# A decoder trunk of two layers: where the value projection's last groups are computed around the RWKV-7 recurrence

## The reference

```python
r = xr @ w_r;  k = xk @ w_k;  v = xv @ w_v          # 256x2048 @ 2048x2048 each
decay = exp(-exp(w_log));  g = sigmoid(xg @ g1) @ g2
def step(state, (r, w, k, v, a, b)):                # 32 heads of 64 channels, 256 tokens
    state = state * w + (state @ a) b^T + v k^T
    return state, state @ r
y = group_norm(scan(step)) + bonus(r, k, v)
out = (y * g) @ w_o
```

## Time and profile before

| | us |
|---|---|
| median of 3 runs | 2485.27 |
| lowest and highest | 2484.48 and 2485.36 |
| span of the profiled execution, first to last instruction | 2481.7 |
| TensorE busy in it | 2444.9 |

### The profile page before, as it was taken

How to read it: one execution, slowest core, us unless ns; L and a number is a source line. 1 busy time by engine, 2 the same in 40 slices (tenths; PEclk the granted TensorE clock), 3 DMA queues, 4 the chain that set the end, 5 groups by cost and what they waited for, 6 DMA issues and landing times.

```text
span 2481.7 us, 39434 instructions
## 1 busy us (share of the span) xinstructions
PE 2444.9 (99%) x15550; PEld 2003.2 (81%) x15550; DVE 1410.0 (57%) x1743; ACT 1074.4 (43%) x1347; POOL 126.0 (5%) x166
## 2 busy tenths in 40 slices
PE   8999999999999999999999999999999999999997
PEld 5888788877888888888887788888788888888886
DVE  6688566676744454454446544666745445454445
ACT  4454355444444444443334344453544444443332
POOL 1000235420000000000000000000000000000000
PEclk9999999999999999999999999999999999999999
DMA  7556411255666666665665565445566666666564
GB/s 233 179 195 205 136 42 38 66 208 188 196 192 188 186 193 186 188 188 193 193 195 198 195 193 188 143 167 190 170 187 192 188 186 193 186 194 221 189 194 143
DMA packets 225435, 440.87 MB, mean 178 GB/s; under 512 B 13472, under 2 KB 23744, under 8 KB 224224
## 3 DMA queue, kind: packets, MB, share of 16 engines
q1 hardware_dynamic: 221760, 417.38, 54.1%
q0 software_dynamic: 3552, 21.73, 2.6%
HBM read 436.96 MB, written 2.10 MB: 177 GB/s over the span
## 4 chain that ended last, share of the span: by engine, by line
PE 94%; DVE 3%; ACT 1%; issue 1%; DMA 1%; POOL 0%; DVEq 0%; ACTq 0%; SPq 0%; POOLq 0%
PE ps L595 25%; PE ps L597 25%; PE ps L596 25%; PE ps L892 3%; PE ps L1075 1%; PE ps L775 1%; PE ps L785 1%; PE ps L1103 1%; PE ps L622 1%; PE ps L624 1%; PE ps L623 1%; PE ps L882 1%; PE ps L836 1%; DVE wlo L1684 1%; PE ps L740 1%
## 5 line engine op out<-in xcount | busy, mean ns | idle before, releaser
L1246 ACT CAST whi<-raw 128x1024 fp32r<-128x1024 f32 x735 | 772.5, 1052 | 1145.9 <-PE ps L597 1080.1
L1684 DVE TENSOR_TENSOR wlo<-raw,whi 128x1024 fp32r<-128x1024 f32 x549 | 670.1, 1225 | 622.2 <-ACT whi L1246 620.3
L595 PE MATMUL ps<-whi,ahi 128*128 128x512 f32 x2172 | 851.5, 392 | 2.8 <-DVE wlo L1684 2.8
L597 PE MATMUL ps<-whi,alo 128*128 128x512 f32 x2172 | 845.6, 389 | 0.0
L596 PE MATMUL ps<-wlo,ahi 128*128 128x512 f32 x2172 | 845.1, 389 | 0.0
L595 PEld LDWEIGHTS ps<-whi,ahi 128*128 128x128 f32 x2172 | 407.8, 188 | 87.6 <-DVE wlo L1684 3.6
L597 PEld LDWEIGHTS ps<-whi,alo 128*128 128x128 f32 x2172 | 407.7, 188 | 85.5
L596 PEld LDWEIGHTS ps<-wlo,ahi 128*128 128x128 f32 x2172 | 407.9, 188 | 84.4 <-issue 1.0
L2015 DVE TENSOR_TENSOR wlo<-raw,whi 128x1024 fp32r<-128x1024 f32 x193 | 236.2, 1225 | 249.4 <-ACT whi L1246 247.4
L595 PE MATMUL ps<-whi,hThi 128*128 128x512 f32 x656 | 255.4, 389 | 0.0
L597 PE MATMUL ps<-whi,hTlo 128*128 128x512 f32 x656 | 255.2, 389 | 0.0
(11 more groups left out here) (317 smaller groups left out, 1933.8 us busy)
## 6 DMA issues: line engine op xcount, KB each, us to landing
raw<-w_up SPq DMA_DIRECT2D x176, 512.0 KB, 3.6
raw<-w_down SPq DMA_DIRECT2D x176, 512.0 KB, 4.0
raw<-w_gate SPq DMA_DIRECT2D x170, 512.0 KB, 3.6
raw<-w_k SPq DMA_DIRECT2D x32, 512.0 KB, 3.8
raw<-w_r SPq DMA_DIRECT2D x32, 512.0 KB, 4.4
raw<-w_v SPq DMA_DIRECT2D x32, 512.0 KB, 3.7
raw<-w_o SPq DMA_DIRECT2D x32, 512.0 KB, 4.8
raw<-kv_v SPq DMA_DIRECT2D x32, 512.0 KB, 3.7
```

The source lines that it names most:

```text
L595: mm(o, hi[:, k, tok], whi[:, s, k2, :], start=(k == 0), stop=False)
L597: last = mm(o, lo[:, k, tok], whi[:, s, k2, :], start=False, stop=(k == kt - 1))
L1246: nc.scalar.copy(whi[:, s], src).then_inc(hi_done, 1)
L1684: V.tensor_tensor(wlo[:, s], src, whi[:, s].bitcast(F32), ALU.subtract).then_inc(split_done, 1)
```

## The change

SOLID becomes 3: a third job in the split form makes value groups 4 and 5 ahead of the recurrence. It takes job number 10 of a phase that is planned with 12 jobs but only 11 jobs' chunks. The counts on the two pairs of banks are evened out by a signal from ScalarE's first Exp of the decays. EARLY becomes 6, so 2 value groups and 8 gate groups remain in plain units: 96 in place of 160. The 20 units ahead of slot 0 stay; the 76 in the slots are dealt out anew, where 140 were. Slot 7 keeps its row. The copies out of bank 3 move to the places that fit the new order.

```diff
--- before.py
+++ after.py
@@ -40,7 +40,7 @@
 KC = 2
 RING = 4
 PLAIN = 3
-SOLID = 2
+SOLID = 3
 FK = 4
 FU = FK * 2
 CJ = KT // KC
@@ -51,19 +51,19 @@
 CHUNK = 64
 PAIRS = D // P
 GROUPS = PAIRS // 2
-EARLY = GROUPS // 2
+EARLY = 2 * SOLID
 LATE = GROUPS - EARLY
-TURNS = [("value", 4), ("value", 5), ("gate", 0), ("gate", 1), ("value", 6), ("value", 7)] + [("gate", g) for g in range(2, GROUPS)]
+TURNS = [("value", 6), ("gate", 0), ("gate", 1), ("value", 7)] + [("gate", g) for g in range(2, GROUPS)]
 UNITS = {"value": KT * TT, "gate": 2 * TT}
-SOME = {"state1": 2, "inner3": 1, "outer3": 2, "outer4": 2, "inner5": 3, "outer5": 4}
+SOME = {"state1": 1, "inner3": 1, "outer3": 1, "outer4": 1, "inner5": 1, "outer5": 2}
 FILL = (
-    {"inner1": 3, "outer1": 2, "inner2": 2, "state1": 3, "inner3": 2, "outer3": 3, "outer4": 2, "inner5": 3, "outer5": 4},
-    SOME,
-    {"state1": 1, "inner3": 1, "outer3": 2, "outer4": 2, "inner5": 4, "outer5": 4},
+    {"outer1": 1, "inner2": 1, "state1": 2, "inner3": 2, "outer3": 3, "outer4": 3},
+    {"outer3": 2, "inner5": 2},
+    {"state1": 1, "outer3": 1, "outer4": 2, "inner5": 2, "outer5": 2},
     SOME,
     SOME,
-    {"state1": 2, "inner3": 2, "outer3": 3, "outer4": 2, "inner5": 3, "outer5": 4},
-    {"inner1": 2, "outer1": 2, "inner2": 2, "state1": 4, "inner3": 2, "outer3": 4, "outer4": 4, "outer5": 4},
+    SOME,
+    {"state1": 2, "inner3": 1, "outer3": 2, "outer4": 2, "outer5": 4},
     {"inner1": 4, "outer1": 2, "inner2": 2, "state1": 2, "inner3": 2, "outer3": 2, "inner4": 2, "outer4": 2, "inner5": 2},
 )
 WHOLE = 4
@@ -118,11 +118,11 @@
 
 PH = {}
 _c = _j = 0
-for _name, _jobs, _per in (("proj", 10, CJ), ("wo", NJ, CJ), ("up0", 2 * FB, CJ), ("down0", NJ, CF), ("kvq", 12, CJ),
+for _name, _jobs, _per in (("proj", 12, CJ), ("wo", NJ, CJ), ("up0", 2 * FB, CJ), ("down0", NJ, CF), ("kvq", 12, CJ),
                            ("ao", NJ, CJ), ("up1", 2 * FB, CJ), ("down1", NJ, CF)):
     assert _c % RING == 0 and _j % 2 == 0
     PH[_name] = (_c, _j)
-    _c += _jobs * _per - (WHOLE if _name == "wo" else 0)
+    _c += _jobs * _per - {"proj": CJ, "wo": WHOLE}.get(_name, 0)
     _j += _jobs
 CHUNKS = _c
 LANDED = {PH[n][0] + RING + e: e for n in ("up0", "kvq", "up1") for e in range(PLAIN)}
@@ -992,8 +992,10 @@
                 job(c + CJ, j // 2, 1, KT, ahi, alo)
                 if n < 2:
                     jobs(c + 2 * CJ, j + 2, NJ - 2, KT, ahi, alo)
+                else:
+                    job(c + 2 * CJ, j // 2 + 1, 0, KT, ahi, alo)
             for b in range(2):
-                pe.wait_ge(bank_free[b], 6)
+                pe.wait_ge(bank_free[b], 7)
             transposes_of(0)
             fill(6)
             for a in range(2):
@@ -1291,7 +1293,9 @@
                 if g:
                     act.wait_ge(nat_done, g)
                 ci = ps[:, 4].rearrange("p (t c) -> p t c", t=TT)
-                A(PC[:, g % 3].rearrange("p l c -> p (l c)"), ps[:, 6, 0:8], ACT.Exp)
+                first = A(PC[:, g % 3].rearrange("p l c -> p (l c)"), ps[:, 6, 0:8], ACT.Exp)
+                if g == 0:
+                    first.then_inc(bank_free[1], 1)
                 A(E[:, 0], ci, ACT.Exp)
                 A(E[:, 1], ci, ACT.Exp, scale=-1.0).then_inc(cum_read, 1)
 
@@ -1335,8 +1339,8 @@
             project_first(0, K_, {1: 0, 2: 1})
             project_first(1, R_, {0: 2, 1: 3})
             project_first(2, V_, {})
-            act.wait_ge(bank_free[0], 6)
-            act.wait_ge(bank_free[1], 6)
+            act.wait_ge(bank_free[0], 7)
+            act.wait_ge(bank_free[1], 7)
 
             def turned(g, a):
 
@@ -1436,8 +1440,6 @@
                 outer(s, 2)
                 if s == 7:
                     keep_gate(5)
-                if s in (0, 5):
-                    keep({0: 4, 5: 6}[s])
                 outer(s, 3)
                 if s:
                     outputs(s - 1)
@@ -1449,17 +1451,17 @@
                 if s == 7:
                     for g, bank in ((0, 4), (1, 6), (2, 5)):
                         keep_zt(g, bank)
-                if s in (2, 6):
-                    keep({2: 5, 6: 7}[s])
+                if s in (0, 6):
+                    keep({0: 6, 6: 7}[s])
                 if more:
                     turned(s + 1, 1)
                 if s == 2:
-                    keep_gate(0)
+                    keep_gate(1)
                 outer(s, 5)
                 if more:
                     first(s + 1)
-                if s in (2, 6):
-                    keep_gate({2: 1, 6: 2}[s])
+                if s in (1, 6):
+                    keep_gate({1: 0, 6: 2}[s])
                 if more:
                     for a in (1, 0):
                         value_part(s + 1, a)
@@ -1804,7 +1806,7 @@
             for b, asides in enumerate((parts_of(2), parts_of(3), [lambda: bonus(0), lambda: None, lambda: bonus(1)])):
                 splits(NJ * CJ, b, asides)
             splits_and_mix(2, 3)
-            for b, asides in enumerate(([lambda: None, lambda: None, lambda: bonus(2)], [lambda: bonus(3)])):
+            for b, asides in enumerate(([lambda: None, lambda: None, lambda: bonus(2)], [lambda: bonus(3)], [])):
                 splits(2 * NJ * CJ, b, asides, 4 if b < SOLID - 1 else 2)
 
             def blank(g):
```

## The result

The change makes the kernel slightly slower: 2492.76 us (median of 10 runs, 2490.17 to 2494.40) against 2487.03 us (median of 10), a ratio of 1.0025 with a 95% interval of 1.0017 to 1.0033, that is +4 to +8 us. I had forecast +1.2 us (2486.5) and "same"; the sign of the difference was right, its size was not, and it is clear of no change. The 2486.5 stood on the median of three runs of the kernel before, 2485.27; on the 2487.03 of ten, my +1.2 us would be 2488.2, and the miss is 4.5 us.

What follows compares the result with a forecast made beforehand. TensorE, busy 99% of the span, was taken as the bound. Job +21.8 us less 20.6 given back (of 29.7 removed) made +1.2 us on 2485.27, so 2486.5 us, range 2481 to 2493, "same" at 0.75.

Steps and rivals of the forecast that it cites:

- Added job, 21.8 us: Ahead of the recurrence: third split job, 96 matmuls at 227 ns from start to start, its splits and loads hidden, adds 21.8 us.
- all behind it moves as a block: At the border behind the last half job and after the recurrence: everything shifts together, cost 0, bound 0 to 1.3 us.
- Removed work, 29.7 us: In the recurrence: 64 plain units at 0.43 us plus 11 vanished groups at 0.2 us, 29.7 us of TensorE's time.
- 0.2 us for each of 11 groups: In the recurrence: each group of plain units that vanishes whole saves TensorE 0.2 us beside its units.
- New waits with a releaser, 9.1 us: In the recurrence: of 29.7 us removed, 20.6 is given back and the other 9.1 become short waits of TensorE.
- What I took back for GpSimd: Slots 4 and 5: GpSimd's products for the next group's transposes come late, 0.1 and 0.3 us taken off the gain.
- Two pauses ... taken as unchanged: In runs of small matmuls in the recurrence: TensorE pauses of 1.35 and 0.76 us without releaser stay, bound 2.1 us either way.
- TensorE-bound everywhere: Rival, recurrence: removed work is given back in full, 2477.4 us, or 2482 half way; chance 0.15.
- Clock: Rival: more waits drop TensorE from 2.4 to 1.2 GHz; one slot at the lower level gives 2508 us; chance 0.03.
- The turns: Rival, slot ends (inner5 and outer5): ScalarE and VectorE queues bind, 6.8 us booked there is lost, 2493.3 us; chance 0.15.
- my own signs: Recurrence forecast at 201.8 us; under 197 would mean steps paid for in full, over 206 would mean the turns.
- The 3.6 us between span and time: Whole kernel before: three-run median 2485.27 exceeds the profile's span 2481.7 by 3.6 us, taken as present in every run.

## Why the prediction was wrong

- **Added job, 21.8 us:** 21.2 in the change, 21.4 alone. Right. That all behind it moves as a block: right, 0 at the border and 1979.9 us behind the last outer step in both.
- **Removed work, 29.7 us:** 27.05. The 0.43 us a unit was right (27.5 for 64); the 0.2 us for each of 11 groups was mis-sized. I took the drawn distance between a run of units and its neighbours for a cost, and the work that fell leaves nothing for it. This is 2.65 of the missing 5.9 us.
- **New waits with a releaser, 9.1 us:** 8.2 (1.25 to 9.4). Right in sum, and at the places named: masks at inner 5 and value products behind the copies. The mask wait after inner 5 is 0.29 us in slots 3 to 5; slots 1, 4 and 5 gave, without pauses, 3.0, 2.5 and 3.1 of 2.7, 2.4 and 3.0, slot 3 only 1.9 of 2.5. Not foreseen: the outputs' copy in front of the transposes (0.36 to 0.39 us in each of slots 2 to 5) and the gate copy in slot 2 (0.45); slot 2 gave 0.87 of 1.9. What I took back for GpSimd never came: it isn't named in front of the transposes, ScalarE is.
- **"Two pauses ... taken as unchanged", bound +-2.1 us:** the failed step. They rose by 4.1 us in these profiles, twice the bound, and by 4.4 in the mean over the block positions tried. The new deal was forecast as if what had no releaser had nothing to do with the change. This is the largest part of the miss.
- Sum: 27.05 - 8.2 - 4.1 = 14.7, against 29.7 - 9.1 = 20.6.
- **The rivals.** TensorE-bound everywhere: no, 12 us of idle time appeared. Clock: no. The turns: by my own signs they were to blame, as the recurrence took over 206 us and the loss was 5.9 us, beyond the 3.8 at which they were to decide. They were not: from inner 5 to the next slot's inner 1 slots 3 to 5 took 7.95 us before and 6.8 after, 1.15 to 1.2 us given where 1.15 was booked. A length over a bound did not tell this cause from another.
- **The 3.6 us between span and time** are not "what lies around it in every run": a run's time is 1.9 to 3.6 us above its own span. The forecast difference doesn't hang on it.

Shown: the pauses stand at block borders (in all 14 profiles, of 13 kernels), they end 1.2 to 1.6 us behind the landing of a packet of instructions, they move with the instruction count, and the new deal pays more for them at every position tried. That fast use of instructions brings them is borne out by the count of blocks: 68% of those used up in under 3.3 us end in a pause, 6% of the others. A unit takes 0.43 us for its four instructions, a small matmul 0.03 us for two, and a packet alone 0.9 to 1.4 us. No experiment shows it, since the one meant to (units at outer1 and inner2) moved the pauses too little. The number of fast blocks doesn't explain the size: there are 9 of them in the kernel after and 7 in the one before, but such a block costs 0.72 us in the new deal and 0.38 in the old one, and why stays open.

## What to carry to other kernels

Fillers between the steps of a latency chain have two prices: what their engine pays for them, and what they hide; compare release and start at each place, and don't take the distance between two drawn runs for a cost. Long runs of very short instructions can stop for their own next block: count the instruction numbers of waits without a releaser before taking them as noise, and repeat a comparison of under half a per cent with the stream shifted by some instructions, reading from the trace by how many it really moved. Where a program is unrolled, a change that makes the chain tighter also makes it ask for instructions faster, and that is the first place to look for a gain that does not arrive.

## What the runs showed of the hardware that was not expected

- In the recurrence, TensorE's pauses of 0.2 to 1.6 us without a releaser end only at record numbers 193 and 194 modulo 256, up to 10.0 us in a recurrence of 211 us.
- Of 102 such pauses 101 end 1.2 to 1.6 us behind the landing of a 16 KB packet on the instruction queue.
- The same binary has them at the same places with other lengths (2.6 and 3.5 us in two profiles), so part of the spread of the timed runs (5 us) may be theirs; this wasn't tried.
- Adding 64 waits at the start (32 records), with no other change, moved the recurrence by +3.4 us (before) and +3.1 (after).
- Waits of TensorE on a semaphore that is long set stand two to a record, and such records follow each other at 0.108 us: 192 waits took 10 us, outlasted the first loads and put the first matmul 2.4 us later (11.36 instead of 8.93 us).
